# Strassen gate tiles: x loaded into the homes of its operand sums and scaled on ScalarE, VectorE's order changed

## The chip, the cores and the metric

The kernel runs on 1 core of one Trainium2 chip. The metric is the device time of one execution in microseconds, as the median of the runs taken.

## The reference, cut to what matters

One layer of a hybrid decoder for 520 tokens (512 of a prompt and 8 samples): h = RMSNorm(x), one input projection of h, two token mixers, per-channel sigmoid gates, an output projection, and an MLP. The change touches only the last of the gate tiles:

```python
z = rmsnorm(x, g_mix_norm) @ w_in            # ..., g_a, g_b are its last 2 x 2048 columns
mix = jax.nn.sigmoid(g_a) * (o_a @ w_proj_gmlp) + jax.nn.sigmoid(g_b) * (o_b @ w_proj_nsa)
x = x + mix @ w_out
```

Everything is float32. The kernel multiplies in the fp32r type with each operand split into a high and a low part and three products (high by high, high by low, low by high).

## The kernel before, in words

**Layout.** All activations lie transposed, features on the 128 partitions and the 520 tokens along the free dimension, in two halves of 260 (`HT`). A weight block of 128 output features is loaded into `w_raw` (four slots) by SyncE's DMA queue. ScalarE rounds it into `w_hi`, VectorE subtracts into `w_lo`, and TensorE multiplies both with `a_hi` and `a_lo`, the parts of x times `g_mix`. The factor `rstd` of the norm is applied to the result (VectorE). So each piece of weight passes DMA, ScalarE, VectorE and TensorE, and each engine takes its work strictly in the order in which it is written out.

**Straight gate units.** There are 16 pairs of gate tiles (one of g_a, one of g_b). The first 9 (`M_ST`) are made straight, as units (m, 0) and (m, 1) with m from 0 to 8 (`NH` is 8). A unit is four chunks of weights (`CH`); `beside(u, jobs)` on ScalarE and VectorE makes the four chunks of the next unit and runs one job behind each. Heads 0 to 7 of the attention run beside the units of m = 0 to 7: scores, softmax, turning the probabilities, the product with the values, and the spatial mixing of one channel group (`turn_group`, `mix_group`, `group_mixed`). `gate_out` multiplies a finished tile with `rstd` (VectorE) and takes its tanh (ScalarE). GpSimd finishes it (`gate_half`) and stores it to `merge_d`.

**Strassen gate pairs.** The last 7 pairs (`N_ST`) use a Strassen-Winograd product: a pair is a 2x2 of 128 output features by 260 tokens, over 8 pairs of input tiles (`KP`), with 7 products instead of 8. A product is 24 matmuls of 260 columns (`st_product`, L1244), so a pair is 168 and the stage 1176. The products of a pair are numbered b = 0 to 6.
- On the token side, tiles 2j and 2j+1 of x give four sums (`st_blocks(j)`, L2358 to L2367: one VectorE instruction over two sums, then two over one each), which lie in the second plane of `st_f[j]`. `st_hi(j)` on ScalarE rounds them into the first plane of the same home `st_t[j]` (L1638), then `st_lo(j)` on VectorE puts the low parts over the sums (L2373). Product 2 is the first that reads them; products 0 and 1 read `a_hi` and `a_lo` alone.
- x itself comes again from memory: GpSimd loads tiles 2j and 2j+1 by one DMA of 520 KB into one of two buffers `xs` (L2981), and multiplies each tile with `g_mix` (L2988, 16 instructions in all). `xs_next(j)` waits until the sums of an earlier j have been read out of the buffer.
- On the weight side, `st_sums(p, n)` with n = 0 to 3 makes the sums of pair p in place in `w_raw` or in `st_sum` (L2424, L2428, L2430, L2434), and `ring_in(p, k)` with k = 0 to 6 brings one block into a ring of three: the high part on ScalarE (L1665), the low part on VectorE (L2415). TensorE starts product b when `ff_lo` has counted `ring_in(p, b)`.
- On the output side, `st_copy` and `st_c21` (ScalarE, L1676, L1681) and `st_added(p, n)` (VectorE, L2443) bring the PSUM banks together; product 3 waits until `st_added(p, 0)` has read its bank. `st_scale` (VectorE, L2449) and `st_tanh` (ScalarE, L1685) finish the tiles of the pair before.

**The order around the change.** It is written out by hand on each engine. On VectorE, the sums j = 0 to 4 lie in the jobs of units (7, 0), (7, 1) and (8, 0). After them comes: `gate_out(8, 0)`, `st_lo(4)`, `st_blocks(5)`, `ring_in(p, 0)`, `st_lo(5)`, `st_blocks(6)`, `st_sums(p, 0)`, `st_lo(6)`, `st_blocks(7)`, `gate_out(8, 1)`, `ring_in(p, 1)`, `st_lo(7)`, and then `st_pair` for each pair (L2464). SyncE refills slot 2 of `w_raw` when `ring_in(p, 3)` has been counted, slot 1 after `st_sums(p, 3)`, slot 0 after `ring_in(p, 4)` and slot 3 after `ring_in(p, 6)`.

## Time and profile before

| | |
|---|---|
| median of 3 runs | 2682.11 us (2681.99, 2682.11, 2684.76) |
| profiled execution, its own time | 2684.72 us |
| its span | 2683.3 us |
| mean granted TensorE clock | 0.997 |
| busy: TensorE / weight loads / VectorE / ScalarE / GpSimd | 2649.3 / 2615.8 / 1942.0 / 1375.1 / 488.9 us |
| DMA | 374.19 MB, mean 139 GB/s |

The profiled execution is 2.6 us over the median of the runs. The span runs from the first to the last instruction, and the remaining 1.4 us lie around it. "Idle before" is the time for which an engine did nothing before an instruction, with the instruction that released it. A clock of 1.00 is the full 2.4 GHz.

### The profile page before, as it was taken

Reading aid. Unit: us, or ns where it says so; the run is one execution under the profiler, and the core shown is the slowest. Engines: PE = TensorE matmul, PEld = TensorE weight load, DVE = VectorE, ACT = ScalarE, POOL = GpSimd, SP = SyncE. Lnnn points to the kernel's source line nnn. Section 1 sums busy time; section 2 is a strip of 40 time slices with the busy share of each in tenths; the row PEclk is TensorE's granted clock in tenths of the full one; section 3 lists DMA queues with packets and bytes.
Section 4 is the critical chain, followed back from the end, with each engine's and each line's share of the span. In section 5 each row is a group of like instructions: output and inputs, shape, how many; then the busy total and the mean of one; then the engine's idle time right before and its main releaser. Section 6 shows DMA issues by size and latency. Waiting matters only on the chain. (4 is left out here: it accounts for less than half of the span.)

```text
span 2683.3 us, 59463 instructions
## 1 busy us (share of the span) xinstructions
PE 2649.3 (99%) x21867; PEld 2615.8 (97%) x21867; DVE 1942.0 (72%) x3125; ACT 1375.1 (51%) x2396; POOL 488.9 (18%) x635
## 2 busy tenths in 40 slices
PE   9999999999998999999999999999999999999998
PEld 9999999999997999999999999999999999999998
DVE  6455655655556775445669988888988889888888
ACT  6435433444443453222246666666666666656656
POOL 2001232200015221003311112112112112111113
PEclk9999999999998999999999999999999999999999
DMA  6533233322223335434435566566566566566578
GB/s 222 180 102 111 86 125 105 118 90 79 75 90 115 119 121 164 136 126 138 135 107 149 143 169 166 143 167 168 144 171 158 152 168 161 149 167 155 155 170 179
DMA packets 123939, 374.19 MB, mean 139 GB/s; under 512 B 13922, under 2 KB 15602, under 8 KB 123584
## 3 DMA queue, kind: packets, MB, share of 16 engines
q1 hardware_dynamic: 69328, 245.36, 27.5%
q0 software_dynamic: 51344, 122.00, 21.5%
q10 hardware_dynamic: 3168, 5.45, 0.6%
q8 instruction: 69, 1.13, 0.2%
q14 instruction: 30, 0.25, 0.0%
HBM read 288.05 MB, written 91.00 MB: 141 GB/s over the span
## 5 line engine op out<-in xcount | busy, mean ns | idle before, releaser
L1936 DVE TENSOR_TENSOR w_lo<-w_raw,w_hi 128x512 fp32r<-128x512 f32 x336 | 241.0, 719 | 465.1 <-ACT w_hi L1433 464.5
L2574 DVE TENSOR_TENSOR w_lo<-w_raw,w_hi 128x1024 fp32r<-128x1024 f32 x352 | 430.4, 1225 | 107.7 <-ACT w_hi L1761 106.5
L1433 ACT ACTIVATE w_hi<-w_raw 128x512 fp32r<-128x512 f32 x336 | 210.8, 629 | 536.4 <-PE mm L877 516.2
L1761 ACT ACTIVATE w_hi<-w_raw 128x1024 fp32r<-128x1024 f32 x352 | 370.8, 1062 | 204.6 <-PE aux L1292 62.6
L877 PE MATMUL mm<-a_hi,w_hi 128*128 128x260 f32 x2176 | 449.9, 288 | 0.2 <-issue 0.2
L877 PE MATMUL mm<-a_hi,w_lo 128*128 128x260 f32 x2176 | 438.2, 283 | 0.0
L877 PE MATMUL mm<-a_lo,w_hi 128*128 128x260 f32 x2176 | 437.4, 283 | 0.0
L1292 PE MATMUL aux<-at_t,w_hi 128*128 128x260 f32 x2304 | 417.1, 283 | 0.5 <-DVE w_lo L2574 0.4
L1292 PEld LDWEIGHTS aux<-at_t,w_hi 128*128 128x128 f32 x2304 | 355.1, 188 | 1.4 <-issue 1.0
L1352 PE MATMUL aux<-fb_mid,w_hi 128*128 128x260 f32 x1920 | 352.2, 283 | 1.4 <-DVE w_lo L2574 1.1
L877 PEld LDWEIGHTS mm<-a_hi,w_hi 128*128 128x128 f32 x2176 | 335.3, 189 | 6.5 <-issue 5.3
L877 PEld LDWEIGHTS mm<-a_lo,w_hi 128*128 128x128 f32 x2176 | 335.3, 188 | 0.0
L877 PEld LDWEIGHTS mm<-a_hi,w_lo 128*128 128x128 f32 x2176 | 335.1, 188 | 0.0
L1292 PE MATMUL aux<-at_t,w_lo 128*128 128x260 f32 x1152 | 325.6, 283 | 0.0
L1352 PEld LDWEIGHTS aux<-fb_mid,w_hi 128*128 128x128 f32 x1920 | 296.0, 188 | 2.9 <-DVE w_lo L2574 1.3
L1352 PE MATMUL aux<-fb_mid,w_lo 128*128 128x260 f32 x960 | 271.4, 283 | 0.0
L1352 PE MATMUL mm<-fb_mid,w_hi 128*128 128x260 f32 x1440 | 265.1, 283 | 0.0
L1292 PE MATMUL mm<-at_t,w_hi 128*128 128x260 f32 x1280 | 232.8, 282 | 1.6 <-DVE w_lo L2574 1.1
L1352 PEld LDWEIGHTS mm<-fb_mid,w_hi 128*128 128x128 f32 x1440 | 222.4, 189 | 0.0
L1292 PEld LDWEIGHTS aux<-at_t,w_lo 128*128 128x128 f32 x1152 | 217.0, 188 | 0.0
L3091 POOL TENSOR_TENSOR cell<-cell 128x1 f32<-128x1 f32 x62 | 20.7, 334 | 1061.5 <-ACT y_mid L1812 1049.7
L1352 PE MATMUL mm<-fb_mid,w_lo 128*128 128x260 f32 x720 | 204.0, 283 | 0.0
(461 smaller groups left out, 5344.8 us busy)
## 6 DMA issues: line engine op xcount, KB each, us to landing
w_raw<-in_w_ff SPq DMA_DIRECT2D x256, 512.0 KB, 3.9
w_raw<-in_w SPq DMA_DIRECT2D x170, 512.0 KB, 3.8
out_y_t<-y_mid POOLq DMA_DIRECT2D x120, 520.0 KB, 8.1
w_raw<-in_w_st SPq DMA_DIRECT2D x28, 512.0 KB, 4.2
g_in<-merge_d POOLq DMA_DIRECT2D x16, 520.0 KB, 5.0
merge_d<-z POOLq DMA_DIRECT2D x26, 260.0 KB, 2.4
xs<-in_x_t POOLq DMA_DIRECT2D x8, 520.0 KB, 4.2
pages<-in_cache_cmp POOLq DMA_DIRECT2D x16, 256.0 KB, 3.2
```

What stands on the lines that cost most here:

```text
L877: last = pe.matmul(mm[:, 2 * v + h, 0:HT], w, a[:, kt, h * HT:(h + 1) * HT], start=first and k == 0 and part == 0, stop=final and k == CK ...
L1292: last = pe.matmul(dst, w, at_t[:, j, e:e + HT], start=FRESH[b] and j == 0 and part == 0, stop=j == KP - 1 and part == 2, skip_group_check ...
L1352: last = pe.matmul(dst, w, fb[:, j, e:e + HT], start=FRESH[b] and j == 0 and part == 0, stop=j == 1 and part == 2, skip_group_check=not FR ...
L1433: run(w_hi[:, c, :], raw(u, c), ACT.Copy).then_inc(hi_split, 1)
L1761: run(hi_of(p, k), source(p, k), ACT.Copy).then_inc(ff_hi, 1)
L1936: dve.tensor_tensor(w_lo[:, c, :], raw(u, c), w_hi[:, c, :].bitcast(F32), ALU.subtract).then_inc(lo_split, 1)
L2574: dve.tensor_tensor(lo_of(p, k), source(p, k), hi_of(p, k).bitcast(F32), ALU.subtract).then_inc(ff_lo, 1)
L3091: pool.tensor_tensor(cell[:, 2:3], cell[:, 0:1], cell[:, 1:2], ALU.mult).then_inc(cell_step, 1)
```

## The change

The two buffers `xs` go. Tiles 2j and 2j+1 of x are loaded straight into the first plane of `st_f[j]` (`st_x(j)`), by two DMAs of 260 KB, each in two runs of 260 elements for a partition. The homes of j are dealt out anew, in the order in which the tensors that lie there are done with, and a few tensors of the attention move up by 128 bytes to make room. GpSimd only issues the loads: each waits for the tensor in its home and for the load before it. ScalarE scales x in place (`st_scaled(j)`, two instructions of 128x520). On VectorE the sums and low parts change their places among the jobs, `st_sums(p, 1)` and `st_sums(p, 2)` come ahead of `ring_in(p, 2)`, `st_scale(old, 1)` comes behind `ring_in(p, 4)`, `st_added(p, 1)` ahead of the next pair's block 0, and the next pair's block 1 at the end of this pair. ScalarE's order is fitted to it.

```diff
@@ -384,12 +384,13 @@
         junk = at("junk", [P, 8, HD], r2 + 4096)
-        wm = at("wm", [P, GRP, P], r2)
-        b_bc = at("b_bc", [P, GRP, P], r2 + 4096)
-        pt_long = at("pt_long", [P, 2, NCH, P], r2 + 8192)
-        pt_short = at("pt_short", [P, 2, 2, P], r2 + 12288)
-        pt_cmp = at("pt_cmp", [P, 2, P], r2 + 14336)
-        assert r2 + 15360 <= r2_end
+        r2b = r1b + 32 * HT
+        wm = at("wm", [P, GRP, P], r2b)
+        b_bc = at("b_bc", [P, GRP, P], r2b + 4096)
+        pt_long = at("pt_long", [P, 2, NCH, P], r2b + 8192)
+        pt_short = at("pt_short", [P, 2, 2, P], r2b + 12288)
+        pt_cmp = at("pt_cmp", [P, 2, P], r2b + 14336)
+        assert r2 <= r2b and r2b + 15360 <= r2_end
         r3 = top[0]
@@ -424,13 +425,12 @@
         g_size = 32 * HT
-        st_home = [i2, i2 + g_size, i1, i1 + g_size, i2 + 4 * g_size, i2 + 2 * g_size, i2 + 3 * g_size, i2 + 5 * g_size]
+        st_home = [i2, i1, i2 + g_size, i2 + 2 * g_size, i1 + g_size, i2 + 4 * g_size, i2 + 5 * g_size, i2 + 3 * g_size]
         st_t = [at(f"st_t{j}", [P, 4, 2, HT], st_home[j], F32R) for j in range(KP)]
         st_f = [at(f"st_f{j}", [P, 4, 2, HT], st_home[j]) for j in range(KP)]
-        xs = [at("xs0", [P, 2, TOK], i2 + 47424), at("xs1", [P, 2, TOK], f1 + 4 * (P + 3 * TOK))]
         z_odd = [at("z_odd0", [P, TOK], i1 + 2 * g_size), at("z_odd1", [P, TOK], i2 + 6 * g_size)]
         st_sum = at("st_sum", [P, BW], f1 + 4 * (P + 2 * TOK))
-        assert i1 + 2 * g_size + 4 * TOK <= r1 and xs[0] is not None
+        assert i1 + 2 * g_size + 4 * TOK <= r1
@@ -642,12 +642,14 @@
-        XS_OF = (1, 1, 0, 1, 0, 1, 0, 1)
         T_INDEX = {T1: 0, T3: 1, T2: 2, T4: 3}
...
+        def st_x(j):
+            return st_f[j][:, :, 0, :]
@@ -1632,6 +1634,14 @@
+            def st_scaled(j):
+                for k in range(2):
+                    act.wait_ge(xs_loaded[k], 16 * j + 16)
+                    x = st_x(j)[:, 2 * k:2 * k + 2, :]
+                    last = run(x, x, ACT.Copy, scale=g_mix[:, 2 * j + k:2 * j + k + 1])
+                last.then_inc(xs_scaled, 1)
@@ -1643,8 +1653,12 @@
                         jobs[1] = lambda: (load_bias(h + 1), copy_queries(h + 1))
-                    if w == 1 and not ahead:
-                        jobs[1] = lambda: st_hi(0)
+                    if not ahead and w == 0:
+                        jobs[0] = lambda: st_scaled(0)
+                        jobs[3] = lambda: st_hi(0)
+                    if not ahead and w == 1:
+                        jobs[1] = lambda: (st_scaled(1), st_scaled(2))
+                        jobs[3] = lambda: st_hi(1)
                     beside((U_GATE // 2 + h, w), jobs, first=lambda: exps(a, w))
@@ -1652,7 +1666,9 @@
             head(NH - 1, False)
-            beside((U_GATE // 2 + NH, 0), [None, lambda: st_hi(2), lambda: st_hi(3)], first=lambda: st_hi(1))
+            beside((U_GATE // 2 + NH, 0), [lambda: st_scaled(3), lambda: (st_hi(3), st_scaled(4)),
+                                           lambda: (st_hi(4), st_scaled(5)), lambda: st_scaled(6)],
+                   first=lambda: st_hi(2))
             gate_out(NH, 0)
@@ -1685,13 +1701,12 @@
             p = Pair(0)
-            st_hi(4)
+            st_hi(5)
+            st_scaled(7)
             ring_in(p, 0, (chunk_done, CH * (U_PROJ - 1) + 2))
-            st_hi(5)
             st_hi(6)
+            st_hi(7)
             ring_in(p, 1, (chunk_done, CH * U_PROJ))
-            gate_out(NH, 1)
-            st_hi(7)
@@ -1699,19 +1714,21 @@
                 ring_in(p, 2, None if old else (chunk_done, CH * U_PROJ))
+                if not old:
+                    gate_out(NH, 1)
                 st_copy(p, 0)
                 ring_in(p, 3)
+                ring_in(p, 4)
                 if old:
                     st_tanh(old, 0)
-                ring_in(p, 4)
-                if old:
-                    st_tanh(old, 1)
                 if end:
...
                 ring_in(p, 5)
+                if old:
+                    st_tanh(old, 1)
                 st_copy(p, 2)
@@ -2357,14 +2374,11 @@
-                x, f = xs[XS_OF[j]], st_f[j][:, :, 1, :]
+                x, f = st_x(j), st_f[j][:, :, 1, :]
                 dve.wait_ge(xs_scaled, j + 1)
-                if j < 2:
-                    dve.wait_ge(v_stored, 16)
-                    dve.wait_ge(v_copied, NH // 2 * (j + 1))
-                steps.did(dve.tensor_tensor(f[:, 0:2, :], x[:, :, HT:TOK], halves(x[:, 0, :]), ALU.subtract))
-                steps.did(dve.tensor_tensor(f[:, 2, :], x[:, 1, HT:TOK], f[:, 0, :], ALU.subtract))
-                dve.tensor_tensor(f[:, 3, :], x[:, 1, 0:HT], f[:, 2, :], ALU.subtract).then_inc(st_src, 1)
+                steps.did(dve.tensor_tensor(f[:, 0:2, :], x[:, 1:4:2, :], x[:, 0:2, :], ALU.subtract))
+                steps.did(dve.tensor_tensor(f[:, 2, :], x[:, 3, :], f[:, 0, :], ALU.subtract))
+                dve.tensor_tensor(f[:, 3, :], x[:, 2, :], f[:, 2, :], ALU.subtract).then_inc(st_src, 1)
@@ -2404,9 +2418,10 @@
                 head(h)
-            head(NH - 1, [[None, None, None, lambda: st_blocks(0)], [None, lambda: st_lo(0), None, lambda: st_blocks(1)]])
-            beside((U_GATE // 2 + NH, 0), [lambda: (st_lo(1), st_blocks(2)), lambda: (group_mixed(NH - 1), st_lo(2)),
-                                           lambda: st_blocks(3), lambda: (st_lo(3), st_blocks(4))])
+            head(NH - 1, [[None, lambda: st_blocks(0), None, lambda: st_lo(0)],
+                          [None, None, lambda: st_blocks(1), lambda: (st_blocks(2), st_lo(1))]])
+            beside((U_GATE // 2 + NH, 0), [lambda: (st_lo(2), st_blocks(3)), lambda: (group_mixed(NH - 1), st_lo(3)),
+                                           lambda: st_blocks(4), lambda: (st_lo(4), st_blocks(5))])
             gate_out(NH, 0)
@@ -2449,46 +2464,48 @@
             p = Pair(0)
-            st_lo(4)
-            st_blocks(5)
-            ring_in(p, 0)
             st_lo(5)
             st_blocks(6)
+            ring_in(p, 0)
+            st_blocks(7)
+            st_lo(6)
             st_sums(p, 0)
-            st_lo(6)
-            st_blocks(7)
+            st_lo(7)
+            st_sums(p, 1)
+            ring_in(p, 1)
             gate_out(NH, 1)
-            ring_in(p, 1)
-            st_lo(7)
...
                 if old:
-                    ring_in(p, 1)
-                st_sums(p, 1)
+                    st_sums(p, 1)
+                    st_sums(p, 2)
+                ring_in(p, 2)
                 if old:
                     st_scale(old, 0)
-                ring_in(p, 2)
-                st_sums(p, 2)
-                if old:
-                    st_scale(old, 1)
+                else:
+                    st_sums(p, 2)
                 ring_in(p, 3)
...
                 ring_in(p, 4)
+                if old:
+                    st_scale(old, 1)
                 if end:
...
                 ring_in(p, 6)
-                if not end:
-                    ring_in(Pair(p.n + 1), 0)
-                    st_sums(Pair(p.n + 1), 0)
                 st_added(p, 1)
...
                     lo((U_PROJ // 2, 0), 1)
+                else:
+                    ring_in(Pair(p.n + 1), 0)
+                    st_sums(Pair(p.n + 1), 0)
                 st_added(p, 2)
+                if not end:
+                    ring_in(Pair(p.n + 1), 1)
@@ -2978,47 +2995,36 @@
             def xs_load(j):
-                pool.dma_start(xs[XS_OF[j]][:, :, :], t["x_t"][2 * j:2 * j + 2].rearrange("k p n -> p k n")
-                               ).then_inc(xs_loaded[XS_OF[j]], 16)
-            def xs_scale(j):
-                pool.wait_ge(xs_loaded[XS_OF[j]], 16 * XS_OF[:j + 1].count(XS_OF[j]))
                 for k in range(2):
-                    x = xs[XS_OF[j]][:, k, :]
-                    last = pool.tensor_scalar(x, x, g_mix[:, 2 * j + k:2 * j + k + 1], None, ALU.mult)
-                last.then_inc(xs_scaled, 1)
-            def xs_next(j):
-                pool.wait_ge(st_src, j - 1)
-                xs_load(j)
+                    if j:
+                        pool.wait_ge(xs_loaded[k], 16 * j)
+                    pool.dma_start(st_x(j)[:, 2 * k:2 * k + 2, :], t["x_t"][2 * j + k].rearrange("p (h c) -> p h c", h=2)
+                                   ).then_inc(xs_loaded[k], 16)
...
                     gate_half(m, p, z[:, p, :])
+            pool.wait_ge(v_stored, 16)
+            pool.wait_ge(v_copied, NH // 2)
             xs_load(0)
...
             gate_half(NH - 2, 1, z[:, 1, :])
-            xs_scale(0)
             gate_half(NH - 1, 0, z[:, 0, :])
-            pool.wait_ge(st_src, 1)
+            pool.wait_ge(scored, 6 * NH)
             xs_load(1)
-            pool.wait_ge(scored, 6 * NH)
-            pool.wait_ge(s_max, 6 * NH)
+            pool.wait_ge(v_copied, NH)
             xs_load(2)
-            xs_scale(1)
-            xs_scale(2)
-            xs_next(3)
+            pool.wait_ge(p_turned, 6 * NH)
+            xs_load(3)
+            pool.wait_ge(aux3_made, 4 * NH - 1)
+            xs_load(4)
             gate_half(NH - 1, 1, z[:, 1, :])
-            xs_scale(3)
-            xs_next(4)
-            xs_next(5)
-            xs_scale(4)
-            xs_next(6)
-            xs_scale(5)
+            xs_load(5)
+            pool.wait_ge(aux3_made, 4 * NH)
+            xs_load(6)
+            pool.wait_ge(u_mixed, NH)
+            xs_load(7)
             gate_half(NH, 0, z[:, 0, :])
-            xs_next(7)
-            xs_scale(6)
-            xs_scale(7)
             gate_half(NH, 1, z[:, 1, :])
...
```

## Rows read from the trace of the kernel before

**Rows 1.** The page, part 1: busy time, share of the span and count of each engine.

```profile
PE 2649.3 (99%) x21867; PEld 2615.8 (97%) x21867; DVE 1942.0 (72%) x3125; ACT 1375.1 (51%) x2396; POOL 488.9 (18%) x635
```

**Rows 2.** Waits of TensorE, 700 to 1060 us: total, times, longest.

```profile
PE aux L1244 <- DVE w_lo L2415: 10.7, 2, 6.8
PE aux L1244 <- DVE z L2443: 4.8, 4, 1.9
PE mm L1244 <- DVE z_odd L2443: 1.5, 1, 1.5
```

**Rows 3.** Timeline of TensorE: start, length, what, count, idle before.

```profile
844.35 0.39 PE L1244 MATMUL aux<-a_hi,w_hi 128*128 128x260 f32 x1 [3.92 <-DVE w_lo L2415]
...
855.63 0.59 PE L1244 MATMUL aux<-a_hi,w_hi 128*128 128x260 f32 x1 [6.78 <-DVE w_lo L2415]
...
865.94 0.59 PE L1244 MATMUL aux<-st_t,w_hi 128*128 128x260 f32 x2 [1.90 <-DVE z L2443]
...
879.06 0.28 PE L1244 MATMUL mm<-a_hi,w_hi 128*128 128x260 f32 x1
...
881.95 0.28 PE L1244 MATMUL mm<-a_hi 128*128 128x260 f32 x1
...
1007.99 0.48 PE L877 MATMUL mm<-a_hi,w_hi 128*128 128x260 f32 x2 [0.17 <-issue]
```

**Rows 4.** Windows, TensorE alone: length, busy (matmuls), granted clock, DMA share, GB/s.

```profile
855.63:860.30 4.67, 4.67 (x24) 0.60 0.15 57
910.40:914.40 4.00, 3.91 (x20) 0.57 0.93 257
975.10:979.10 4.00, 3.95 (x33) 1.00 0.85 321
```

**Rows 5.** Timeline of VectorE: start, length, what, idle before.

```profile
841.24 0.70 DVE L2365 TENSOR_TENSOR st_f<-xs 128x520 f32<-128x520 f32 x1 [1.48 <-POOL xs L2988]
...
897.53 1.23 DVE L2415 TENSOR_TENSOR a_lo<-w_raw,a_hi 128x1024 fp32r<-128x1024 f32 x1 [3.96 <-ACT a_hi L1665]
...
908.79 1.22 DVE L2434 TENSOR_TENSOR st_sum<-w_raw,st_sum 128x1024 f32<-128x1024 f32 x1
909.93 0.42 DVE L2443 TENSOR_TENSOR z<-z,aux 128x260 f32<-128x260 f32 x1
```

**Rows 6.** The buffers xs: shortest, median, longest ns, first and last start.

```profile
L2988 POOL TENSOR_SCALAR xs<-xs,gains x16: 1573/1839/2636, 780.7 to 849.6; 128x520 f32<-128x520 f32 x16
L2981 POOL DMA_DIRECT2D xs<-in_x_t x8: 716/728/766, 743.5 to 843.5; - x8
...
DMA to landing us min/median/max: 4.1/4.2/5.1
```

**Rows 7.** The homes st_f: shortest, median, longest ns, first and last start.

```profile
L2365 DVE TENSOR_TENSOR st_f<-xs x8: 686/694/702, 796.6 to 852.2; 128x520 f32<-128x520 f32 x8
L2366 DVE TENSOR_TENSOR st_f<-xs,st_f x8: 429/430/806, 797.3 to 852.9; 128x260 f32<-128x260 f32 x8
...
L1638 ACT ACTIVATE st_t<-st_f x8: 1053/1065/1074, 806.9 to 855.0; 128x1040 fp32r<-128x1040 f32 x8
L2373 DVE TENSOR_TENSOR st_t<-st_f,st_t x8: 1226/1238/1725, 808.8 to 856.1; 128x1040 fp32r<-128x1040 f32 x8
```

**Rows 8.** Timeline of GpSimd, 700 to 900 us: the second load.

```profile
801.24 0.73 POOL L2981 DMA_DIRECT2D xs<-in_x_t  x1
```

**Rows 9.** DMA issues from 780 to 1010 us: count, KB each, median us to landing.

```profile
merge_d<-z POOLq DMA_DIRECT2D x11, 260.0 KB, 4.6
```

**Rows 10.** The copy of v for a head, on ScalarE: shortest, median, longest ns.

```profile
L1619 ACT ACTIVATE v_g<-v_t x8: 622/622/625, 542.5 to 804.0; 128x520 f32 x6, 128x520 f32<-128x520 f32 x2
```

**Rows 11.** Timeline of TensorE: the last product with the values, in unit (7, 1).

```profile
813.63 1.50 PE L1186 MATMUL aux<-pt_long,v_row 128*128 128x128 f32 x12
```

**Rows 12.** Timeline of ScalarE, 780 to 900 us.

```profile
830.01 0.62 ACT L1433 ACTIVATE w_hi<-w_raw 128x512 fp32r<-128x512 f32 x1
...
896.44 1.06 ACT L1665 ACTIVATE a_hi<-w_raw 128x1024 fp32r<-128x1024 f32 x1 [2.20 <-DMA w_raw<-in_w_st]
```

## Prediction

> **What bounds the kernel now.** I read the page first: TensorE is busy for 99% of the span [rows 1]. Only its idle time can be won, and slow matmuls that hide in the busy time. The list of its waits shows where: in the Strassen gate stage it waits 17 us, 10.7 of them in two pieces for a low part of weights (L2415), and 6.3 in five pieces for `st_added(p, 0)` (L2443) ahead of product 3 [rows 2]. The timeline of TensorE gives the places: 3.92 us before product 0, 6.78 before product 1, 1.90 before product 3 of the first pair [rows 3]. A product at full speed takes 881.95 - 879.06 = 2.89 us [rows 3]. The windows show what waits leave behind: the 24 matmuls after the 6.78 us took 4.67 us at a granted clock of 0.60, and after the wait at 910.49 the clock was 0.57, which is 1.2 GHz for most of the stretch, while after the 1.51 us wait it was 1.00 (2.4 GHz) [rows 2 to 4]. So a long wait costs itself and about 1.6 us more.
>
> The stage runs from 844.35 - 3.92 = 840.43 to 1007.99 us: 167.6 us for 49 products, which need 49 x 2.89 = 141.6. **26.0 us is all that can be won.** They fall into three parts:
> - up to product 3 of the first pair: 865.94 - 840.43 = 25.5, less three products, 8.7: 16.8 us;
> - the next four products: 879.06 - 865.94 = 13.1 against 11.6: 1.5 us of slow clock;
> - the other 42: 1007.99 - 879.06 = 128.9 against 121.4: 7.5 us, of which 6.3 - 1.9 = 4.4 are waits for `st_added` and about 1.7 the clock after the one at 910.49 [rows 2 to 4].
>
> Behind the first part stands VectorE. Its timeline shows `st_blocks` waiting 1.48 us for GpSimd's scaling (one of three such waits), with `ring_in` queued behind it [rows 5]. The scaling takes 1.84 us a tile, 29 us in all, the next load waits for its buffer, and beside it VectorE's own instructions stretch: `st_lo` from 1.24 to 1.73 us, the sums from 0.43 to 0.81 [rows 6, 7].
>
> **The change, part by part.**
>
> *Loads.* Seven loads now follow one another from 801.24 us on, when load 1 was issued before [rows 8], each behind its home's last reader and the load before. A load of 520 KB took 4.2 us to land and 0.73 to issue [rows 6]. Two DMAs of 260 KB cost GpSimd 1.46 us. No row shows their landing as a pair. Below: 4.2 as before. Above: 4.6 each, the median of the 260 KB stores in this stretch [rows 9], one behind the other, 9.2. I take 4.2, since the bytes are the same and both are in flight together. Then load 7 is issued at 828 to 830 us, when `group_mixed` and load 6 are done, and is there by 834. Load 0 also waits for the copy of v of head 3, more than 100 us old. `gate_half(7, 1)` and `gate_half(8, 0)` are queued behind loads 4 and 7, but the readers of their stores are over 10 us away. The 128 bytes cost nothing.
>
> The issue is also the place of a rule that speaks against the change: the Trainium skill (SBUF — State Buffer, SBUF: two separate sides) says that VectorE in a two-port mode keeps GpSimd from writing descriptors, so that its DMAs hang. Here the eight issues lie within 716 to 766 ns while VectorE was busy [rows 6]; by the rule 14 issues instead of 7 would be exposed, by the row they cost 0.73 us each. The sum goes by the row.
>
> *Scaling on ScalarE.* 16 instructions of 128x520, at 0.62 us as the plain copy of that size [rows 10]: 9.9 us more on an engine that is busy for 51% of the span [rows 1, 10]. No row shows this copy with a factor for each partition: the width is the same, so 0.62 is the lower end and what I take, and above I allow 1.06, the length of 128x1040 [rows 7]. Five of the eight pairs lie beside the straight units, where ScalarE waits for TensorE. In unit (7, 1) it waits in order for load 2, which lands at about 809; `probs_out` behind it ends near 812, before TensorE comes to it at 813.6 [rows 11], so nothing is lost.
>
> *GpSimd's 29 us of scaling* go, and with them VectorE's waits and stretches.
>
> *First pair.* I lay out the new order with the old durations; back to back, an instruction of 1.22 us is followed after 1.14 [rows 5]. In unit (8, 0) ScalarE gets three `st_hi` and four `st_scaled`; its last chunk, before at 830.01 [rows 12], slips to 831.3. Then VectorE: low part to 832.6, `st_lo(4)` 833.7, `st_blocks(5)` (0.69 + 0.43 + 0.43) 835.2, `gate_out` 835.8. ScalarE: tanh to 836.5, `st_hi(5)` 837.5, `st_scaled(7)` 838.5, block 0 (1.05 [rows 12]) 839.5. VectorE: `st_lo(5)` 837.5 to 838.7, `st_blocks(6)` 840.2, block 0 841.4. **Product 0 starts at 841.4 in place of 844.35.** VectorE goes on with `st_blocks(7)` (1.5) and five instructions of 1.15 (`st_lo(6)`, sums 0, `st_lo(7)`, sums 1, block 1): **product 1 at 848.6 in place of 855.63**, since TensorE has waited 848.6 - 844.3 = 4.3 us. After that wait I charge the slow 4.67 us: 853.3. Meanwhile VectorE does `gate_out(8, 1)`, block 2 (850.3), sums 2 (851.4), waits for ScalarE's block 3 (852.4), low part 853.6, sums 3 854.8, `st_added(p, 0)` 855.1. Product 2 runs 853.3 to 856.2, so **product 3 starts at 856.2 in place of 865.94: 9.7 us won**, and 1.5 for its slow clock. `gate_out(8, 1)` is later in both queues, but GpSimd's store of it lands by about 856, and ScalarE's copy that waits for it comes at 859.
>
> *Later pairs.* From block 0 to `st_added` the old order took 909.93 + 0.42 - 897.53 = 12.8 us in pair 2 [rows 5]. The new one strings 8 instructions at 1.14 (block 0, sums 0, block 1, sums 1, sums 2, block 2, block 3, sums 3), one `st_scale` at 0.6, and two additions at 0.34: 10.7 us. Two waits of 0.5 for ScalarE go too, since a sum now covers each of its copies, and that is in the 10.7. 2.1 us won is more than the longest wait, 1.90, so all four go, and their slow clock with them. What I move back is covered: `st_scale(old, 1)` and `st_tanh(old, 1)` come about 5 us later, and their tile's buffer is wanted a pair later (20 us); for the last one `load_gates` may start 3 us later and its reader has about 5 us. SyncE's loads start as much earlier as blocks 3 and 4 are done. Of the 7.5 us I keep 0.2, the step into the projections.
>
> **Sum:** 9.7 + 1.5 + 7.3 = 18.5 us. Against the profiled execution's own 2684.7 this is 2666.2; that execution lies 2.6 us over the median, so against the median of 2682.1 it is **2663.6 us**. About 0.2% (5.4 us) is what a measurement of this kernel can tell from no change.
>
> **Rivals.**
>
> *The pairs keep their waits.* Before the longest of them ScalarE waited 2.20 us for the DMA of slot 0 [rows 12]; if the DMA sets block 0, the order behind it may not matter. Against it: 10.7 us of chain fit after the same block 0, and slot 0 is now refilled earlier. Only 11.2 us are won: 2670.9 us. Chance 0.13.
>
> *ScalarE becomes the bound.* Its in-order queue holds scaling, high parts and copies. If all 9.9 us lay on the path, 8.6 would be left: 2673.5 us. Chance 0.09.
>
> *VectorE's own work is the bound,* and the change does not do what it says: the sums still stand ahead of `ring_in`, and only what was waiting for GpSimd goes, 1.48 three times and about 2 us of stretch, of which the clock may eat some. Within 5 us of before, say 2679 us. Chance 0.05.
>
> *Slower: the chain of loads.* `st_scaled(7)` stands ahead of ScalarE's block 0, and product 3 follows it by 856.2 - 837.5 = 18.7 us. If the two DMAs of a load run one behind the other at 4.6 us, seven loads end at 801.2 + 7 x 9.2 = 865.6, and product 3 starts at about 884.3. The gain is 0 when load 7 lands at 837.5 + 18.5 = 856.0, which is 7.8 us a load; at 9.2 the kernel is 9.6 us slower: 2691.7 us. For it: every load waits for the one before. Against it: 4.2 us for the same bytes [rows 6]. The Trainium skill (DMA: Bandwidth & Descriptors, Anatomy of one DMA — SWDGE (gpsimd) path) gives a DMA a fixed 2.0 us plus its bytes at 436 GB/s, so that two halves pay the fixed part twice; by that estimate the two halves take 5.2 us end to end, load 7 is there at about 838, and the forecast would lose under 1 us. Chance 0.04.
>
> **Numbers.** Chances: forecast 0.69, pairs keep their waits 0.13, ScalarE 0.09, VectorE 0.05, loads 0.04. The forecast's own spread is 2659.5 (of the 26.0 us only 3.4 left) to 2668. The range goes up to 2672.5 to take in the first rival and part of the second, and leaves out less than 2 in 10. Faster by over 0.2%: 0.69 + 0.13 + 0.09 = 0.91; within: 0.05; slower: 0.04.
>
> **What would show it.** Right: TensorE idle about 1 us before product 0, about 4 before product 1 with a clock near 0.6 behind it, and no wait for L2443's successor in the pairs; the scaling on ScalarE at about 0.62 us; VectorE's `st_lo` at 1.24 throughout; loads landing in about 4 us. Wrong: ScalarE waiting for the loads beside `st_scaled`; waits ahead of product 3 left in pairs 2 to 6; a new wait of TensorE in head 7; or more than 6 us idle in the first pair.

## The result, and the profile after

The changed kernel takes 2665.25 us (median of 4 runs, 2664.03 to 2666.92). The kernel before took 2682.7 us in the same session (4 runs, 2681.99 to 2684.76). The ratio is 0.9934, with a 95% interval of 0.9917 to 0.9951. So it is faster, by 17.4 us where 18.5 were forecast, and 2665.25 lies in the range of 2659.5 to 2672.5. The profiled execution took 2666.92 us (span 2665.5, mean clock 0.999) and is the slowest of the four.

Part 1 of the page, against [rows 1]:

```profile
PE 2643.3 (99%) x21867; PEld 2611.1 (98%) x21867; DVE 1937.7 (73%) x3125; ACT 1385.0 (52%) x2412; POOL 458.3 (17%) x627
```

The share of TensorE is 99% as before, and its busy time fell by 6.0 us for the same 21867 matmuls: slow matmuls went, not matmuls. ScalarE has 16 instructions and 9.9 us more, GpSimd 30.6 us less.

The waits of TensorE from 700 to 1060 us, against [rows 2]: total, times, longest.

```profile
PE aux L1246 <- DVE w_lo L2430: 5.4, 2, 4.1
```

Before, the same view had one piece more than [rows 2] show, 0.5 us ahead of product 2 of the first pair (at 860.89). Of these 17.5 us in eight pieces, 5.4 us in two are left. No wait for `st_added` (now L2458) stands in the list. The timeline of TensorE gives the places, against [rows 3]:

```profile
841.36 0.39 PE L1246 MATMUL aux<-a_hi,w_hi 128*128 128x260 f32 x1 [1.36 <-DVE w_lo L2430]
...
848.61 0.39 PE L1246 MATMUL aux<-a_hi,w_hi 128*128 128x260 f32 x1 [4.09 <-DVE w_lo L2430]
...
853.00 0.51 PE L1246 MATMUL aux<-st_t,a_hi 128*128 128x260 f32 x2
...
988.42 0.48 PE L879 MATMUL mm<-a_hi,w_hi 128*128 128x260 f32 x2
```

Product 0 starts at 841.36, product 1 at 848.61, product 2 at 853.00, product 3 at 855.99 (the first start of `aux<-st_t,w_hi`, 856.0 in the view of `st_t`). The stage ends at 988.42, where it ended at 1007.99. The windows of TensorE (length, busy, granted clock, DMA share, GB/s), against [rows 4]:

```profile
841.30:844.30 3.00, 2.94 (x24) 1.00 0.03 8
848.60:853.20 4.60, 4.59 (x25) 0.63 0.00 0
853.20:856.10 2.90, 2.90 (x26) 1.00 0.66 229
```

After 1.36 us of idling the clock stayed at full speed; after 4.09 us the next 24 matmuls ran for the most part at the lower level and took 4.4 us in place of 2.9. This is the only slow stretch left in the stage.

What lies in the homes of x (shortest, median, longest ns, first and last start), against [rows 6, 7], with the idle time ahead of these instructions and the landing of the loads:

```profile
L3001 POOL DMA_DIRECT2D st_f<-in_x_t x16: 704/716/737, 743.2 to 831.2; - x16
L1642 ACT ACTIVATE st_f<-st_f,gains x16: 712/715/731, 784.6 to 837.9; 128x520 f32<-128x520 f32 x16
...
L2380 DVE TENSOR_TENSOR st_f<-st_f x8: 428/429/431, 790.2 to 842.0; 128x260 f32<-128x260 f32 x8
...
L2387 DVE TENSOR_TENSOR st_t<-st_f,st_t x8: 1232/1234/1242, 796.5 to 845.0; 128x1040 fp32r<-128x1040 f32 x8
its engine sat idle before it (us, times) until:
  DMA st_f<-in_x_t: 7.2, 2
...
DMA to landing us min/median/max: 3.0/3.3/5.4
```

The longest `st_lo` fell from 1725 to 1242 ns and the longest sum at L2380 from 806 to 431 ns: nothing stretches any more. The scaling takes 0.715 us, not 0.62. The 7.2 us are GpSimd's, ahead of loads 6 and 7, which wait for the load before; ScalarE never waited for x.

VectorE's timeline through the first pair:

```profile
840.09 1.22 DVE L2430 TENSOR_TENSOR w_lo<-w_raw,w_hi 128x1024 fp32r<-128x1024 f32 x1
...
847.34 1.22 DVE L2430 TENSOR_TENSOR w_lo<-w_raw,w_hi 128x1024 fp32r<-128x1024 f32 x1
...
852.55 1.23 DVE L2430 TENSOR_TENSOR w_lo<-w_raw,w_hi 128x1024 fp32r<-128x1024 f32 x1 [1.12 <-ACT w_hi L1681]
...
854.83 0.42 DVE L2458 TENSOR_TENSOR z<-z,aux 128x260 f32<-128x260 f32 x1
```

From block 0 (840.09) to block 1 (847.34) it is never idle. What keeps TensorE waiting 4.09 us ahead of product 1 is VectorE's own work: seven instructions lie between the two blocks.

**What the trace does not settle:** that the 9.6 us won from product 3 to the end of the stage (142.05 to 132.43) came from VectorE's order and not from an earlier refill of `w_raw`, and how much of the rest belongs to the loads and how much to ScalarE. That is what the runs are for.

### The profile page after: what moved, and what is told of

Its sections match the earlier page's. It is cut to its first block and busy times, and to the rows that moved or that the text cites. A ratio compares the mean times of both kernels' runs of the same rounds, so it can differ in the third digit from the quotient of the medians.

```text
span 2665.5 us, 59475 instructions
## 1 busy us (share of the span) xinstructions
PE 2643.3 (99%) x21867; PEld 2611.1 (98%) x21867; DVE 1937.7 (73%) x3125; ACT 1385.0 (52%) x2412; POOL 458.3 (17%) x627
## 3 DMA queue, kind: packets, MB, share of 16 engines
q8 instruction: 69, 1.13, 0.2%
```

## The experiments

Each number is the median of its runs, and the ratio is to the kernel before, which ran beside it in the same session. The changed kernel (2665.25 us) was measured in the first session alone. The median of the kernel before lay between 2681.18 and 2683.19 us in the four sessions, so a difference to the changed kernel is sure to about 1 to 2 us only, and the waits in the traces have to bear it out.

**1. The old order of the pairs, with the new loads and the new first pair.** `st_pair` is that of the kernel before for pairs 1 to 6, on VectorE and ScalarE; the first of VectorE's lines:

```diff
                 if old:
-                    st_sums(p, 1)
-                    st_sums(p, 2)
+                    ring_in(p, 1)
+                    st_sums(p, 1)
+                    st_scale(old, 0)
                 ring_in(p, 2)
+                st_sums(p, 2)
                 if old:
-                    st_scale(old, 0)
+                    st_scale(old, 1)
...
                 ring_in(p, 4)
-                if old:
-                    st_scale(old, 1)
```

> The changed kernel with only the order of pairs 1 to 6 put back on VectorE and ScalarE (block 1 at the head of a pair, sums 2 and both st_scale between the blocks, added 1 behind the next block 0). My theory: the first pair stays as changed (product 0 at about 841.4 us, product 1 at 848.6, product 3 at 856.0), and waits for st_added(p, 0) ahead of product 3 come back in some of the pairs, 3 to 5 us in all, with 0 to 2 us of slow clock: 2668.5 to 2672 us, in the middle 2670. Rival (the DMA of slot 0 had set the waits, and the order does not matter): no wait, 2665 us.

Measured: 2671.75 us (5 runs, 2670.83 to 2672.91), against 2681.82 for before; ratio 0.9963 (0.995 to 0.9977). The waits of TensorE in the stage:

```profile
PE aux L1246 <- DVE w_lo L2430: 5.4, 2, 4.1
PE aux L1246 <- DVE z L2458: 3.5, 3, 1.5
PE mm L1246 <- DVE z_odd L2458: 1.7, 2, 1.4
```

The first pair is as in the changed kernel, and the waits for `st_added` are back, 5.2 us in five pieces. So the order of the pairs is worth 6.5 us beside the new first pair. But ScalarE waited for the DMA of slot 0 in five pairs. In the kernel before it had done so in four (2.20 us, the one of [rows 12], then 0.39, 1.42 and 0.45). Two of the five, from its timeline, and the wait of TensorE that follows the second:

```profile
884.76 1.06 ACT L1681 ACTIVATE a_hi<-w_raw 128x1024 fp32r<-128x1024 f32 x1 [1.40 <-DMA w_raw<-in_w_st]
...
948.62 1.06 ACT L1681 ACTIVATE a_hi<-w_raw 128x1024 fp32r<-128x1024 f32 x1 [1.35 <-DMA w_raw<-in_w_st]
```

```profile
962.67 0.48 PE L1246 MATMUL mm<-st_t,a_hi 128*128 128x260 f32 x2 [1.44 <-DVE z_odd L2458]
```

In the changed kernel it waits for the DMA of no block between 855 and 988 us. The new order removes both waits together, so this run alone can't say which of the two sets product 3.

**2. The scaling back on GpSimd, in the new homes.** `st_scaled` on ScalarE is emptied, and GpSimd gets `xs_scale(j)` (two instructions with `g_mix`) behind the loads:

```diff
             xs_load(7)
+            xs_scale(5)
+            xs_scale(6)
+            xs_scale(7)
             gate_half(NH, 0, z[:, 0, :])
```

> The changed kernel with the scaling of x back on GpSimd, in place in the new homes; loads, homes and orders as changed. My theory: GpSimd's 16 scalings at about 1.84 us again pace the sums: the last is done at about 845 us, product 0 starts at 844 to 845 in place of 841.4, product 1 at about 852.5 in place of 848.6, and the pairs stay without waits, so 3.5 to 5 us are lost: about 2669.5 us. Rival (the reorder alone gave the gain and the engine that scales does not matter): product 0 at 841.4, 2665 us. Rival (GpSimd's scaling was all of the first pair's loss): 9 us or more lost, 2674 us or more.

Measured: 2672.32 us (6 runs, 2671.1 to 2673.9), ratio 0.9966 (0.9953 to 0.9978): 7.1 us slower than the changed kernel, where 4.2 were expected. The timeline of TensorE, and the scaling as the view of `st_f` has it:

```profile
849.37 0.58 PE L1246 MATMUL aux<-a_hi,w_hi 128*128 128x260 f32 x1 [9.30 <-DVE w_lo L2425]
...
856.91 0.39 PE L1246 MATMUL aux<-a_hi,w_hi 128*128 128x260 f32 x1 [1.97 <-DVE w_lo L2425]
```

```profile
L3003 POOL TENSOR_SCALAR st_f<-st_f,gains x16: 1572/1732/2823, 780.4 to 845.8; 128x520 f32<-128x520 f32 x16
...
L2375 DVE TENSOR_TENSOR st_f<-st_f x8: 428/576/1100, 790.3 to 850.0; 128x260 f32<-128x260 f32 x8
```

GpSimd takes 1.57 to 2.82 us for what ScalarE does in 0.72, and VectorE's sums stretch up to 1.10 us. The first of the scalings at 837.37 took 1.57 us while VectorE stood idle (until 840.54), so most of the length is GpSimd's own. I put the extra 3 us down to where I placed the work, which no run tried otherwise: `xs_load(7)` waits for load 6 to land, and `xs_scale(5)` was queued behind it, so the last six scalings could only start at 837.37 and ran to 848.32, where about 845 was expected. No wait is left in pairs 1 to 6: the order of the pairs does its part without the move to ScalarE.

**3. The kernel before with only the new order of the pairs.** `st_pair` on VectorE and the places of `st_tanh` on ScalarE are those of the changed kernel (for the first pair `st_sums(p, 1)` stays inside); loads, scaling and first pair are those of before.

> The kernel before with only the new order of the pairs on VectorE and ScalarE; x is loaded and scaled as before. My theory: product 0 at 844.4, product 1 at 855.6 and product 3 of the first pair at 865.9 as before, no wait for st_added in pairs 1 to 6, so 5 to 7.5 us won: about 2676 us. Rival (DMA sets block 0 of the pairs): waits of 1 to 2 us stay in pairs 2 and 5, under 3 us won: 2680 us or more.

Measured: 2676.92 us (11 runs, 2675.79 to 2679.01) against 2681.82, ratio 0.9981 (0.9972 to 0.999): 4.9 us. The waits of TensorE, against [rows 2]:

```profile
PE aux L1244 <- DVE w_lo L2415: 10.5, 2, 6.6
PE aux L1244 <- DVE z L2443: 1.5, 1, 1.5
```

The 1.5 us are product 3 of the first pair; none is left in pairs 1 to 6, and ScalarE waits for the DMA of no block. From product 3 of the first pair to the end of the stage this execution took 998.40 - 865.59 = 132.8 us, against 1007.99 - 865.94 = 142.05 in [rows 3] and 988.42 - 855.99 = 132.4 in the changed kernel. So this stretch gave 9.2 us between two single executions, 1.5 of them the slow clock behind product 3 of the first pair, and the whole kernel 4.9 between medians. In part that is the profiled execution of before, which lies 2.6 us over its median; the rest is scatter that these runs do not resolve.

**4. Only the two sums of a pair back behind block 2.**

```diff
                 if old:
                     st_sums(p, 1)
-                    st_sums(p, 2)
                 ring_in(p, 2)
+                st_sums(p, 2)
                 if old:
                     st_scale(old, 0)
-                else:
-                    st_sums(p, 2)
```

> The changed kernel with st_sums(p, 2) put back behind block 2, the rest as changed. My theory: VectorE waits again 0.5 to 1.1 us for ScalarE's copy of block 2, so st_added(p, 0) ends about 1 us later; in the changed kernel it ended 1.6 us ahead of product 3, so TensorE still doesn't wait: 2665 to 2666 us. Rival (this piece is what removed the waits): waits ahead of product 3 in several pairs, 2667 us or more.

Measured: 2668.67 us (5 runs, 2667.3 to 2670.43), ratio 0.9953 (0.994 to 0.9967). My expectation missed, and the rival's held: waits of 0.77 us (pair 2) and 1.41 us (pair 5) ahead of product 3 came back.

```profile
PE mm L1246 <- DVE z_odd L2458: 1.4, 1, 1.4
PE aux L1246 <- DVE z L2458: 0.8, 1, 0.8
```

In ScalarE's timeline the wait for slot 0 is back in three pairs (the third, 0.27 us, in pair 6):

```profile
883.58 1.06 ACT L1681 ACTIVATE a_hi<-w_raw 128x1024 fp32r<-128x1024 f32 x1 [1.03 <-DMA w_raw<-in_w_st]
...
945.74 1.06 ACT L1681 ACTIVATE a_hi<-w_raw 128x1024 fp32r<-128x1024 f32 x1 [1.67 <-DMA w_raw<-in_w_st]
...
```

I had counted only VectorE's own chain, from its block 0 to the end of `st_added(p, 0)`. That one came out about as expected: 12.47 us against 11.34 in the changed kernel, where pair 2 shows it, and 12.82 in the kernel before [rows 5].

```profile
883.43 1.22 DVE L2430 TENSOR_TENSOR a_lo<-w_raw,a_hi 128x1024 fp32r<-128x1024 f32 x1 [0.52 <-ACT a_hi L1681]
...
894.35 0.42 DVE L2458 TENSOR_TENSOR z<-z,aux 128x260 f32<-128x260 f32 x1
```

But the refills of `w_raw` hang on VectorE's own counts. When its chain ends later, they start later, and the next pair's block 0 comes later still. This made a theory that could be tested: VectorE's order and the refill feed each other, and the new order has room for a late refill while the old has none.

**5 and 6. The refill of slot 0 one block later, with the new order and with the old.** The same edit on the changed kernel and on the kernel of experiment 1:

```diff
-                for n, (signal, count) in ((2, (ff_lo, p.e + 4)), (1, (ff_sum, p.sums + 4)), (0, (ff_lo, p.e + 5)),
+                for n, (signal, count) in ((2, (ff_lo, p.e + 4)), (1, (ff_sum, p.sums + 4)), (0, (ff_lo, p.e + 6)),
```

> The kernel after with one edit: SyncE refills slot 0 of w_raw one block later, after ring_in(p, 5) in place of ring_in(p, 4), about 3 us later in each pair. In the kernel after the refill for pair 2 could start when VectorE's block 4 was done, 874.61 + 1.23 = 875.8, and lands about 4.2 us later, at 880; ScalarE's block 0 starts at 882.35, so there are 2.3 us to spare. One block later it starts at 877.68 + 1.23 = 878.9 and lands at about 883.1, so ScalarE waits some 0.8 us for it. My theory: the new order of VectorE has 1.6 us to spare ahead of product 3 (added0 ends that much before product 3 may start), so this lateness is taken up and TensorE still waits for nothing in pairs 1 to 6; 2665 to 2667 us. Rival, the DMA of slot 0 alone sets the pairs, and the new order only helps by an earlier refill: the lateness comes out ahead of product 0 or 3 in most of the six pairs, waits of 0.5 to 1 us in each, 2668 to 2672 us.

> The same edit on the kernel with the old order of the pairs (e1_old_pair_order, 2671.75 us), where ScalarE already waits 0.2 to 1.4 us for slot 0 and TensorE 0.3 to 1.5 us ahead of product 3 in five pairs. My theory: there nothing is to spare, neither in the transfer nor in VectorE's order, so the whole 2.9 us of a later refill comes out ahead of product 3 of each pair: waits of about 3 us or more six times, 18 us in all, and some of slow clock behind each: 2688 to 2700 us. Rival, the transfer and the order are independent, and each pair's lateness is taken up as in the new order: under 2675 us.

Measured, new order: 2665.79 us (4 runs, 2665.31 to 2666.7), ratio to before 0.9943 (0.9927 to 0.996). ScalarE now waits 1.16 to 1.55 us for slot 0 in four pairs, and TensorE waits for nothing in pairs 1 to 6. The first of the four, and all waits of TensorE in the stage:

```profile
884.68 1.06 ACT L1681 ACTIVATE a_hi<-w_raw 128x1024 fp32r<-128x1024 f32 x1 [1.55 <-DMA w_raw<-in_w_st]
```

```profile
PE aux L1246 <- DVE w_lo L2430: 5.5, 2, 4.1
PE mm L879 <- ACT z L1697: 1.6, 1, 1.6
```

(The 1.6 us stand at the step into the projections, at 990.66. Slot 0 brings their first weights, which ScalarE now splits at 986.88 in place of 983.98, ahead of `st_c21`; the profile names TensorE as what released it there, so that it was the late slot is read from the edit.) A wait of 1.55 us for slot 0 is more than the 1.40 of experiment 1, and here it costs nothing ahead of product 3. So a late slot 0 by itself does not hold TensorE up; together with the old order it does.

Measured, old order: 2673.26 us (8 runs, 2672.75 to 2675.44), ratio 0.9973 (0.9963 to 0.9984). It is 1.5 us slower than experiment 1, where I expected 16 or more. Five waits for `st_added` add up to 5.1 us, as in experiment 1; 0.9 us more stand at the step into the projections.

```profile
PE aux L1246 <- DVE z L2458: 2.9, 3, 1.2
PE mm L1246 <- DVE z_odd L2458: 2.2, 2, 1.2
PE mm L879 <- ACT z L1697: 0.9, 1, 0.9
```

Two things were wrong in that expectation. In the old order block 5 follows block 4 closely (877.71 and 879.38 on VectorE), so the refill moved by 1.7 us, not 2.9. And the landing did not move with it: from the end of block 3 of pair 1 on VectorE to ScalarE's start on the new slot 0 it is 885.47 - 876.32 = 9.15 us, against 884.76 - 875.34 = 9.42 in experiment 1. Windows of experiment 1 point to a reason (length, then busy time and count of TensorE, weight loads, VectorE, ScalarE, GpSimd; clock, DMA share, GB/s):

```profile
876.00:878.00 2.00, 2.00 (x18) 1.86 (x17) 2.00 (x3) 1.06 (x3) 1.66 (x3) 1.00 0.78 258
878.00:880.00 2.00, 2.00 (x19) 2.00 (x18) 1.39 (x2) 0.37 (x1) 1.25 (x3) 1.00 0.84 152
880.00:882.00 2.00, 2.00 (x19) 2.00 (x18) 0.52 (x1) 1.33 (x2) 0.00 (x0) 1.00 0.92 352
```

The refills of slots 2, 1 and 0 and GpSimd's stores share DMA engines that are 78 to 92% busy from 876 to 882 us and idle from 874 to 876; in the changed kernel the same row of transfers begins 2 us earlier, at 874, since block 3 and sum 3 are done earlier. That what counts is the whole row of refills, and not slot 0's own start, fits both runs but was not tried by itself.

The timelines of five kernels, pair by pair, say more than the medians. Each entry is ScalarE's wait for the DMA of slot 0, then TensorE's wait ahead of product 3 of that pair (us; in pair 1 there is neither):

| | pair 2 | pair 3 | pair 4 | pair 5 | pair 6 |
|---|---|---|---|---|---|
| before (old order) | 2.20, 1.90 | 0, 0 | 0.39, 0.46 | 1.42, 1.51 | 0.45, 0.57 |
| experiment 1 (old order) | 1.40, 1.48 | 0.18, 0.27 | 0.95, 1.04 | 1.35, 1.44 | 0.89, 0.98 |
| experiment 6 (old order) | 1.10, 1.19 | 0.84, 0.94 | 0.65, 0.74 | 1.16, 1.24 | 0.92, 1.01 |
| experiment 4 (one exchange back) | 1.03, 0.77 | 0, 0 | 0, 0 | 1.67, 1.41 | 0.27, 0 |
| experiment 5 (new order) | 1.55, 0 | 1.16, 0 | 0, 0 | 1.50, 0 | 1.54, 0 |

In the old order the lateness of slot 0 comes out whole, and 0.1 us with it, in 13 of 14 pairs (pair 2 of the kernel before is the exception). With one exchange back 0.26 us of it are taken up, and in the new order all of it, up to 1.55 us. So in the old order the DMA sets the size of the waits; no run had the old order with an early slot 0, but these rows leave it only about 0.1 us a pair. The new order does two things: its refills come early enough that ScalarE does not wait, and it has room for one that is late. Experiment 5 shows the second by itself; no run has the first alone.

**7. Each half of a load behind the other.** This is the mechanism of the slower rival:

```diff
-                    if j:
-                        pool.wait_ge(xs_loaded[k], 16 * j)
+                    if j or k:
+                        pool.wait_ge(xs_loaded[1 - k], 16 * (j + k))
```

> The changed kernel with the two halves of a load one behind the other: each DMA of GpSimd waits until the one before has landed. This tests the rival of the slow chain of loads. A half landed in 3.3 us (median) in the changed kernel, so a load takes about 6.8 us and load 7 lands at 801 + 7 x 6.8 = 849 us, where the point of no gain was put at 856. If st_scaled(7) holds block 0 as I reckoned (product 3 of the first pair 18.7 us after load 7 has landed), product 3 starts at about 867 in place of 856, and 11 to 13 us of the gain are gone: about 2677 us, still faster than before. If the loads have slack that I do not see, or the halves land faster alone (2.4 us, 5 us a load): load 7 by 837, under 1 us lost, 2665 to 2666 us.

Measured: 2677.02 us (10 runs, 2676.14 to 2678.37), before of that session 2683.19, ratio 0.9979 (0.997 to 0.9988), as expected. The timeline of TensorE:

```profile
817.77 2.92 PE L1188 MATMUL aux<-pt_long,v_row 128*128 128x128 f32 x12 [4.68 <-DVE pt_long L2365]
...
854.61 0.58 PE L1246 MATMUL aux<-a_hi,w_hi 128*128 128x260 f32 x1 [7.65 <-DVE w_lo L2430]
...
861.86 0.40 PE L1246 MATMUL aux<-a_hi,w_hi 128*128 128x260 f32 x1 [1.68 <-DVE w_lo L2430]
...
868.65 0.48 PE L1246 MATMUL aux<-st_t,w_hi 128*128 128x260 f32 x2 [0.75 <-DVE z L2458]
```

It costs 11.8 us over the changed kernel, and TensorE waits in two places for it: 4.68 us in head 7, where `probs_out` stands behind `st_scaled(2)` on ScalarE, and 7.65 us before product 0. The last half was issued at 848.66 and scaled from 851.62 on, and product 3 follows that by 17.0 us, where the forecast had 18.7. So load 7 sets the first pair, and by this chain the 4.68 us are hardly a cost on top, since the wait before product 0 would be longer without them (no run shows it). The chain of loads is a real risk of this change, and it is the two halves in flight together that keep it off the path.

**8. A version without the long waits.** Since VectorE's own work is what is left before product 1, the work that no early product needs goes behind what it does need:

```diff
-                                           lambda: (st_hi(4), st_scaled(5)), lambda: st_scaled(6)],
+                                           lambda: st_hi(4), lambda: (st_scaled(5), st_scaled(6))],
...
             st_hi(5)
-            st_scaled(7)
             ring_in(p, 0, (chunk_done, CH * (U_PROJ - 1) + 2))
+            st_scaled(7)
...
-            st_lo(5)
             st_blocks(6)
+            st_lo(5)
             ring_in(p, 0)
             st_blocks(7)
             st_lo(6)
             st_sums(p, 0)
-            st_lo(7)
-            st_sums(p, 1)
             ring_in(p, 1)
-            gate_out(NH, 1)
+            st_lo(7)
```

Sums 1 and 2 then come ahead of block 2 in every pair, and `gate_out(NH, 1)` comes behind `st_added(p, 0)` on VectorE and behind block 4 on ScalarE.

> A version that goes on from the changed kernel: ScalarE makes the last weight chunk of unit (8, 0) ahead of st_scaled(5), and block 0 ahead of st_scaled(7); VectorE does st_blocks(6) ahead of st_lo(5), block 1 ahead of st_lo(7), sums 1 and 2 ahead of block 2, and gate_out(8, 1) behind st_added(p, 0). My theory (VectorE's own work and its waits for ScalarE set the first pair): product 0 at 840.1 with no wait, product 1 at 843.4, product 2 at 848, product 3 at 851 to 852 in place of 856.0, with or without a drop of the clock: 4 to 5 us won on the changed kernel, about 2660.5 us. Rival (weights or loads of x hold the first pair): product 3 not before 855, 2665 us. What could spoil it: gate_out(8, 1) is later, so the copy for product 5 may wait for its store.

Measured: 2661.28 us (5 runs, 2660.4 to 2662.01), ratio 0.992 (0.9906 to 0.9933), which is 4.0 us under the changed kernel. The waits of TensorE in the stage:

```profile
PE aux L1246 <- DVE a_lo L2430: 1.5, 1, 1.5
PE aux L1246 <- DVE w_lo L2430: 0.9, 1, 0.9
PE aux L1246 <- ACT z L1692: 0.8, 1, 0.8
```

Product 0 started at 839.62 without a wait, products 1 to 3 at 843.56, 848.20 and 851.18, each within 0.5 us of what was expected. 5.4 us of waiting became 3.2. The granted clock is 1.00 behind each of the three, so the 1.5 us of slow clock go too: 3.7 us by the rows, 4.0 measured. The 0.8 us is the price of the late `gate_out(NH, 1)`: ScalarE's copy waits 4.05 us for its store.

## Why the prediction was right, and where it was not

**First pair, 9.7 us.** Right, and step by step. The order laid out with old durations gave products 0 to 3 at 841.4, 848.6, 853.3 and 856.2; they started at 841.36, 848.61, 853.00 and 855.99, so product 3 came 9.95 us earlier. The scaling was mis-sized: 0.715 us and not 0.62, 11.4 us of busy time in 16 instructions and not 9.9. That cost 0.2 us at most, since only `st_scaled(5)` stood on the path. It puts off the last chunk of unit (8, 0), which ScalarE started at 831.09 where 830.01 had been and 831.3 was forecast. VectorE waited for this chunk, and then for `st_hi(5)`, as laid out:

```profile
831.74 0.69 DVE L1953 TENSOR_TENSOR w_lo<-w_raw,w_hi 128x512 fp32r<-128x512 f32 x1 [2.90 <-ACT w_hi L1435]
...
837.39 1.24 DVE L2387 TENSOR_TENSOR st_t<-st_f,st_t 128x1040 fp32r<-128x1040 f32 x1 [1.67 <-ACT st_t L1648]
```

Block 0 was ready (839.55) when VectorE came to it. Experiment 2 shows what the move was worth with the same loads and the same order on VectorE: 7.1 us, of which about 3 may be due to where the scalings stood.

**Loads.** "4.2 us as before" was the side to take, and still high: the halves landed in 3.3 us in the median. The longest, 5.4 us, was a half of load 6, for which load 7 waited; it was issued at 830.51, half a microsecond behind the 828 to 830 forecast. Two halves one behind the other cost 11.8 us (experiment 7). The rival's path was right, since load 7 then held product 3, and what it had too high was the landing: its 2691.7 us rested on 4.6 us a half, and in experiment 7 they landed in 2.9 to 4.0 us, median 3.1. Load 7 was there at about 851.6; by the rival's sum (no gain at 856.0) that leaves a gain of 4.4 us, and 6.2 were measured. The 5.2 us that the prediction estimated for two halves end to end were too low: load 5 took 837.33 - 830.10 = 7.2 us there from its first issue to the next load's. The issues took 704 to 737 ns, no more than the 716 to 766 of [rows 6], with VectorE busy for 9.3 of the 11.4 us of issuing. The Trainium skill (SBUF — State Buffer, SBUF: two separate sides) would have them held up while VectorE is in a two-port mode; no run here shows that.

**Slow clock after the first pair, 1.5 us.** Right: behind the 1.90 us ahead of product 3 [rows 3] the granted clock had been 0.54 (window in the last section), and with no wait there it is 1.00 from 853.2 us on.

**Pairs 1 to 6, 7.3 us.** Near in sum, and half right in its reason. All waits went. Experiments 1 and 3 put the order of the pairs at 6.5 and 4.9 us between medians, both under the forecast. The rest, 2681.82 - 2671.75 = 10.1 us by experiment 1, was forecast at 9.7 + 1.5 = 11.2. The chain from block 0 to `st_added` was mis-sized for the kernel as it runs: 11.34 us and not 10.7, 1.5 us won and not 2.1, because VectorE still waits 0.52 us for ScalarE's copy of block 3. Only where block 0 comes late, as in experiment 5, does that wait go and the chain take 10.74 (905.49 to 916.23 in pair 3). So for the case that the step reasons about, a block 0 that is late, "2.1 us won is more than the longest wait, so all four go" is borne out by experiment 5, up to 1.55 us of lateness. What the step left out of its sum is that block 0 does not stay where it was: its refill hangs on the chain itself. Experiment 4 gave back 1.13 us of the chain; 0.35 us under the old length were left, slot 0 was late again in three pairs, and two waits came back. The rival "the pairs keep their waits" had the right witness, the 2.20 us before [rows 12]: in the old order slot 0 does set the waits. It had the wrong verdict: experiment 5 has DMA waits of 1.16 to 1.55 us and none of TensorE in the pairs. In the new order `st_added(p, 0)` of pair 1 is done at 874.22 + 0.42 = 874.64, and product 3 starts at 876.1: about 1.5 us to spare, which can take up a late block.

**The sum.** The stage and what leads to it ended 19.6 us earlier (1007.99 to 988.42), where 18.5 were forecast. The time behind it was 1675.3 us before (2683.3 - 1007.99) and 1677.1 after (2665.5 - 988.42), which gives 1.8 us back. Nothing shows that to be an effect of the change: the code there is the same, and in the ten profiled executions of this case it took between 1673.5 us (experiment 7) and 1677.1, in no order that follows the edits. The 19.6 lie between two executions that are 2.6 and 1.7 us over their medians; between the medians it is 17.4. The forecast of 2663.6 and the 2665.25 measured differ by 1.6 us, less than the four runs spread.

**ScalarE and VectorE as the bound.** ScalarE did not become it. The window over the later pairs (columns as in experiment 6) has it busy for 56.03 of 108.42 us:

```profile
880.00:988.42 108.42, 108.39 (x906) 108.21 (x905) 84.36 (x92) 56.03 (x82) 23.11 (x33) 1.00 0.39 130
```

VectorE's own work remains the bound of the first pair, and experiment 8 shows that more than half of what remained there (5.4 us of waits and 1.5 of slow clock) could be had by ordering alone.

## What to carry to other kernels

Lay a new order out instruction by instruction with the durations of the old trace: here this placed four products within 0.3 us each. But when a refill hangs on the counts of the very chain that it feeds, do not hold its landing fixed; work out the next turn with the later start, and ask for room, not only for a sum that comes out positive. When splitting a load, put the two halves in flight together, and look at what is queued behind the consumer's wait on each engine.

## What was unexpected of the hardware

- ScalarE's copy of 128x520 with a factor for each partition takes 0.712 to 0.731 us, against 0.622 for the plain copy of the same size [rows 10].
- Two loads of 260 KB in flight together landed in 3.0 to 5.4 us, median 3.3, where one of 520 KB took 4.1 to 5.1 [rows 6].
- TensorE's clock after a wait: product 3 of the first pair, behind 1.49 us of idling in experiment 3, and behind 1.90 us in the kernel before (ahead of product 1, some 10 us earlier, both had idled 6.6 to 6.8 us; before also had 0.45 us ahead of product 2):

```profile
865.59:868.50 2.91, 2.91 (x24) 1.00 0.89 305
```

```profile
865.94:868.90 2.96, 2.96 (x14) 0.54 0.90 307
```

  In the same length 24 matmuls went through at 2.4 GHz and 14 mostly at 1.2 GHz. Behind 0.83, 0.91, 1.36, 1.48 and 1.50 us the clock was 1.00 too, and behind the 1.68 us of experiment 7; behind the other 1.90 us of the kernel before it was 0.57 [rows 4]. So a few tenths of a microsecond more of waiting went with about 1.5 us of slow clock besides. No run changed this one wait alone.
- GpSimd's scaling of 128x520 takes 1.57 us even while VectorE is idle, where ScalarE takes 0.715 (experiment 2).
- The same refill issued 1.7 us later landed no later, while the DMA engines were about 80 to 90% busy (experiment 6).
